# A fused two-block layer: the front of the first projection begun with three blocks in 48 pieces instead of two in 32, with one PSUM bank shared

## What is computed

```python
sc = jax.nn.silu(c)
scc = jax.nn.silu(c_ctx)
shift, scale, gate = jnp.split(sc @ w_ada[l] + b_ada[l], 3, axis=-1)
shift_c, scale_c, gate_c = jnp.split(scc @ w_ada[l] + b_ada[l], 3, axis=-1)
hc = _rmsnorm(ctx, g_pre[l]) * (1.0 + scale_c) + shift_c
zc = hc @ (w_in[l][:, :XBC_W + DT_W] if last else w_in[l])
xh_c, B_c, C_c, dt_c, A = _ssd_prep(zc, conv_w[l], conv_b[l], dt_bias[l], a_log[l], 1, CTX_LEN)
hx = _rmsnorm(x, g_pre[l]) * (1.0 + scale[:, None]) + shift[:, None]
zx = hx @ w_in[l]
xh, Bm, Cm, dt, A = _ssd_prep(zx, conv_w[l], conv_b[l], dt_bias[l], a_log[l], ROWS, GRID_W)
```

## Time and profile before

| what | value |
|---|---|
| median of 3 runs | 2824.82 us (2823.69 to 2825.59) |
| profiled execution, its own time | 2825.9 us |
| its span, first to last instruction | 2824.1 us |
| PE busy | 2772.1 us (98%), 13174 matmuls |
| VectorE, ScalarE, GpSimd busy | 54%, 39%, 12% |
| DMA | 439.35 MB, mean 156 GB/s |
| first matmul of the body | 165.13 us |
| mean granted TensorE clock | 0.995 of full speed |

### The profile page before, as it was taken

The page is one execution under the profiler, slowest core; times in us unless marked ns, Lnnn a source line. Parts: engine busy times, 40 slices in busy tenths (PEclk is TensorE's granted clock), DMA queues, the critical chain, the costliest instruction groups (busy, mean ns, idle before and its releaser), DMA issues.

```text
span 2824.1 us, 33335 instructions
## 1 busy us (share of the span) xinstructions
PE 2772.1 (98%) x13174; PEld 2245.8 (80%) x13174; DVE 1530.3 (54%) x1834; ACT 1112.1 (39%) x1470; POOL 343.0 (12%) x409
## 2 busy tenths in 40 slices
PE   6999999999999999999999999899999999999999
PEld 2578888888778887888788888788878888788787
DVE  6868667764555546666653233544444444533643
ACT  6742222234343333433333332436555543432611
POOL 0211100000334124322311000100000000000000
PEclk8999999999999999999999999999999999999999
DMA  9657767754455554455455333242222223223252
GB/s 398 245 192 257 250 238 261 256 186 144 142 167 173 164 171 150 148 174 182 143 167 214 112 120 104 86 146 90 82 75 82 83 75 109 78 90 97 96 183 94
DMA packets 162122, 439.35 MB, mean 156 GB/s; under 512 B 14768, under 2 KB 59824, under 8 KB 151728
## 3 DMA queue, kind: packets, MB, share of 16 engines
q1 hardware_dynamic: 123360, 307.28, 32.5%
q0 software_dynamic: 15792, 92.99, 9.3%
q10 hardware_dynamic: 22816, 36.97, 3.7%
HBM read 398.11 MB, written 39.06 MB: 155 GB/s over the span
## 4 chain that ended last, share of the span: by engine, by line
PE 91%; DVE 3%; ACT 3%; issue 2%; DMA 1%; POOL 0%; SPq 0%; DVEq 0%; ACTq 0%
PE PB L413 16%; PE PB L418 15%; PE PB L419 15%; PE PB L522 10%; PE PB L523 10%; PE PB L524 10%; PE PB L416 2%; PE PB L417 2%; PE PB L421 2%; ACT WH L1001 1%; PE PB L639 1%; PE PB L656 1%; PE PB L433 1%; DVE WL L1628 1%; PE PB L886 1%
## 5 line engine op out<-in xcount | busy, mean ns | idle before, releaser
L1628 DVE TENSOR_TENSOR WL<-RAW,WH 128x1024 fp32r<-128x1024 f32 (+1 forms) x424 | 519.5, 1233 | 765.2 <-ACT WH L1001 579.7
L413 PE MATMUL PB<-HH,WH 128*128 128x512 f32 x2048 | 818.9, 400 | 4.1 <-ACT zp L1001 3.7
L418 PE MATMUL PB<-HL,WH 128*128 128x512 f32 x2048 | 802.3, 392 | 0.0
L419 PE MATMUL PB<-HH,WL 128*128 128x512 f32 x2048 | 801.5, 391 | 0.0
L1001 ACT ACTIVATE WH<-RAW 128x1024 fp32r<-128x1024 f32 (+1 forms) x424 | 432.8, 1038 | 434.3 <-PE PB L524 259.8
L522 PE MATMUL PB<-WH,HH 128*128 128x512 f32 x1248 | 490.6, 393 | 0.8 <-DVE HL L1628 0.8
L524 PE MATMUL PB<-WH,HL 128*128 128x512 f32 x1248 | 486.2, 390 | 0.0
L523 PE MATMUL PB<-WL,HH 128*128 128x512 f32 x1248 | 486.1, 390 | 0.0
L413 PEld LDWEIGHTS PB<-HH,WH 128*128 128x128 f32 x2048 | 385.0, 188 | 93.7 <-issue 7.8
L419 PEld LDWEIGHTS PB<-HH,WL 128*128 128x128 f32 x2048 | 385.2, 188 | 67.1
L418 PEld LDWEIGHTS PB<-HL,WH 128*128 128x128 f32 x2048 | 385.6, 188 | 65.5 <-issue 3.4
(11 more groups left out here) (314 smaller groups left out, 2810.0 us busy)
## 6 DMA issues: line engine op xcount, KB each, us to landing
RAW<-in_w_in_t SPq DMA_DIRECT2D x320, 512.0 KB, 3.7
AU<-in_w_ada POOLq DMA_DIRECT2D x64, 1024.0 KB, 5.5
RAW<-in_w_out_t SPq DMA_DIRECT2D x96, 512.0 KB, 3.6
bcb<-R SPq DMA_DIRECT2D x64, 256.0 KB, 6.1
S<-so ACTq DMA_DIRECT2D x24, 384.0 KB, 2.7
ebc<-R SPq DMA_DIRECT2D x32, 256.0 KB, 6.0
SY<-evb ACTq DMA_DIRECT2D x32, 256.0 KB, 2.6
yin<-SY POOLq DMA_DIRECT2D x32, 256.0 KB, 4.3
```

The lines of the kernel that those rows point to most:

```text
L413: h.matmul(banks[j], lh, m.HH[:, t, :], start=st, stop=False)
L418: h.matmul(banks[j], lh, m.HL[:, t, :], start=False, stop=False)
L419: ins = h.matmul(banks[j], ll, m.HH[:, t, :], start=False, stop=en)
L1628: return h.tensor_tensor(o, a, b, op)
```

## The change

The front now begins three blocks without ctx (12, 13, 14) in 48 pieces, 1.5 a beat; the order of blocks becomes 12 to 15, then 0 to 11, so that the last is one with ctx. The first body block is 15, whose first two units are 12 and 13. The six accumulators take banks 0 to 5, the row sums bank 7, and **bank 6 is shared** by fold, x turned and ctx turned, each waiting for what read it last. ctx is turned two tiles at a time, in beats 19, 20, 23, 24, 27, 28, 31 and 35; ScalarE modulates both and splits off the high parts, VectorE makes the low parts, GpSimd none. Early halves are split one beat ahead of use instead of two. SyncE issues 12 raw units among the loads of w_ada, unit u at w_ada tile 6 + 16u/3. The table of places is rewritten to fit. The core of the diff:

```diff
-BLOCKS = (12, 13) + tuple(range(12)) + (14, 15)
-EARLY = 8
+BLOCKS = (12, 13, 14, 15) + tuple(range(12))
+LAST = BLOCKS[15]
+EARLY = 12
...
-    return st, t, k - 20 if 20 <= k < 36 else None, k - 6 if 6 <= k < 6 + 4 * EARLY else None
-BEATS = 6 + 4 * EARLY
+    j = k - 6
+    pieces = range((3 * j + 1) // 2, (3 * j + 4) // 2) if 0 <= j < 32 else range(0)
+    return st, t, {19: 0, 20: 1, 23: 2, 24: 3, 27: 4, 28: 5, 31: 6, 35: 7}.get(k), pieces
+BEATS = 38
...
-    u, tt = divmod(s, 4)
-    return u, tt % 2, tt, 2 * u + tt // 2
+    return s // 4, s % 3, s % 4, s // 3
...
     def fold(st):
+        bank = reuse(6)
         P.wait_ge(*at("rowb", st))
         P.wait_ge(*at("cst"))
-        if st:
-            P.wait_ge(*at("mod", st - 1))
...
-        freed[4] = [("mod", st)]
+        freed[6] = [("mod", st)]
...
+        freed[6] = [("hx", t)]
-    def turn_ctx(t):
+    def turn_ctx(c):
+        bank = reuse(6)
         for v in range(4, 6):
             P.wait_ge(*at("xs", v))
+        for q in range(4):
+            t, v = 2 * c + q // 2, q % 2
+            ins = h.transpose(bank[:, q * 128:(q + 1) * 128], m.xs[4 + v][:, t * 128:(t + 1) * 128], ident)
+        ins.then_inc(*put(P.side, "turn ctx", c))
+        freed[6] = [("hc", 2 * c + 1)]
...
-            if i < 2:
+            if i < 3:
                 continue
...
+    def modulate_ctx(c):
+        A.wait_ge(*at("turn ctx", c))
+        A.wait_ge(*at("Am", c))
+        for t in (2 * c, 2 * c + 1):
+            if t >= 2:
+                A.wait_ge(*at("CL", t - 2))
+            A.then(act(m.hf[t % 2][:, 512:768], m.PB[6][:, t % 2 * 256:t % 2 * 256 + 256], ACT.Identity,
+                       scale=m.Amv[:, t, 1:2], bias=m.modv[:, shift_at(t), 1:2]), "hc", t)
+        place_read(6 * (c // 2) + 4)
+        for t in (2 * c, 2 * c + 1):
+            A.wait_ge(*at("hc", t))
+            A.then(act(m.CH[:, t, :], m.hf[t % 2][:, 512:768], ACT.Copy), "CH", t)
...
-    make(8)
-    make(9)
+        if k in (33, 34):
+            make(k - 21)
...
+    def ctx_low(c):
+        for t in (2 * c, 2 * c + 1):
+            place_read(6 * (t // 4) + 5)
+            V.wait_ge(*at("CH", t))
+            V.then(TT(m.CL[:, t, :], m.hf[t % 2][:, 512:768], m.CH[:, t, :].bitcast(F32), ALU.subtract), "CL", t)
...
     for i in range(64):
-        if i % 8 == 6:
-            raw_load(i // 8)
+        for u in range(EARLY):
+            if i == min(6 + 16 * u // 3, 63):
+                raw_load(u)
```

More of the change, by code:

```diff
@@ L481, in tensor_program @@
             fold(st)
-        if sub is not None:
+        for sub in pieces:
             u, i, tt, t = early_tile(sub)
@@ L564, in tensor_program @@
         with_ctx = b < 12
-        tk = early[i] if i < 2 else [take(ring, "xbc", b, j) for j in range(3 if with_ctx else 2)]
+        tk = early[i] if i < 3 else [take(ring, "xbc", b, j) for j in range(3 if with_ctx else 2)]
         for k4 in range(4):
-            if i < 2:
+            if i < 3:
                 continue
@@ L1062, in scalar_program @@
     for k in range(BEATS):
-        st, t, tc, sub = beat(k)
+        st, t, tc, pieces = beat(k)
         for i in (2 * k, 2 * k + 1):
@@ L1076, in scalar_program @@
                 junk = A.then(act(m.junk, m.xs[v], ACT.Square, acc=m.ss[:, v:v + 1]), "x squared", v)
-        sub = beat(k + 2)[3]
-        if sub is not None and sub % 2 == 0:
-            early_high(sub)
-    make(8)
-    make(9)
+        for sub in beat(k + 1)[3]:
+            if sub % 2 == 0:
+                early_high(sub)
+        if k in (33, 34):
+            make(k - 21)
     def conv_out(i):
@@ L1726, in vector_program @@
                 a_low(i + 2)
+            if tc is not None and i % 2:
+                ctx_low(tc)
             if i in SCALED:
@@ L1730, in vector_program @@
                 V.then(TS(m.xs[v], m.xs[v], m.rr[:, v:v + 1], None, ALU.mult), "xs", v)
-        sub = beat(k + 2)[3]
-        if sub is not None and sub % 2 == 0:
-            early_low(sub)
-    make(8)
-    make(9)
-    for e in ("turn", 15), ("turn ctx", 15), ("HL", 15), ("CL", 15), ("fold", 7):
+        for sub in beat(k + 1)[3]:
+            if sub % 2 == 0:
+                early_low(sub)
+        if k in (33, 34):
+            make(k - 21)
+    for e in ("turn", 15), ("turn ctx", 7), ("HL", 15), ("CL", 15), ("fold", 7):
         V.wait_ge(*at(*e))
@@ L2318, in gpsimd_program @@
         power(rr, "rr", v)
-    for t in range(16):
-        i = max(i for i in range(64) if PLACE[i] == 6 * (t // 4) + 5)
-        G.wait_ge(*at("a hi", i))
-        G.wait_ge(*at("a lo", i))
-        G.wait_ge(*at("CH", t))
-        G.then(h.tensor_tensor(m.CL[:, t, :], m.hf[t % 2][:, 512:768], m.CH[:, t, :].bitcast(F32), ALU.subtract),
-               "CL", t)
-    for e in ("turn", 15), ("turn ctx", 15), ("HL", 15), ("CL", 15), ("fold", 7):
+    for e in ("turn", 15), ("turn ctx", 7), ("HL", 15), ("CL", 15), ("fold", 7):
         G.wait_ge(*at(*e))
@@ L2512, in sync_program @@
             load(m.xs[v], m.x_tile(I, v), s.x[v], "x", v)
-    for u in range(8, 68):
+    for u in range(EARLY, 68):
         raw_load(u)
```

70 lines of the change are left out of this document (25 added, 45 removed).

## The result

| | before | after |
|---|---|---|
| median (6 runs each) | 2824.26 us (2823.69 to 2825.59) | **2836.05 us** (2833.34 to 2848.82) |
| ratio, 95% interval | | 1.0048 (1.0029 to 1.0068) |
| profiled execution, its span | 2825.9, 2824.1 us | 2840.4, 2838.6 us |
| mean granted TensorE clock | 0.995 | 0.990 |

The change makes the kernel slower by 0.48%. The median lies within the range of 2822 to 2840, and on the side to which I had given 0.43, not on that of the likeliest case.

The account below looks back on a forecast made before the run. PE, busy 98% of the span, was taken to bound the kernel. Net +3.7 us at the first ctx block and +1.0 at the stage's end gave +4.7, a forecast median of 2829.5 us, range 2822 to 2840.

Parts of the forecast that it names:

- likeliest case: Whole kernel: hidden 22 us given back in front growth and the wait for unit 14, no difference that shows; chance 0.50.
- rival 2: Front: shared bank binds harder through ScalarE, folds and x's turns wait longer, 9.5 us more, 2839 us; chance 0.36.
- the body's first block: Body start: PE waits 12.2 us on unit 14, ready 24.2 us after first eviction; first ctx block net +3.7 us.
- stages without a gap: Front, fold to fold where PE never idles: six pieces instead of four are paid in full, +2.8 us.
- double ctx beats: Front, fold 5 to 6 and 6 to 7: stages grow to 19.0 to 19.2 us, +2.4 us each.
- fold waits: Front, shared bank: the fold waits 1.1 us for ScalarE's ctx work, at three folds.
- Fold 4 to fold 5: Front stage there: turn waits 2.7 us behind VectorE's scalings, fold 1.1; stage 21.4 to 21.6 us, +3.6.
- the hand-over: Fold 8 to the first eviction: 14.1 us instead of 16.8, -2.7 us, with no gap or clock loss on PE.
- rival 3: SyncE's gated loads land late, each of four gates costs 4 to 5 us: +16 to +20, some 2846; chance 0.07.
- The end of the stage: Last block before dt: three steps of the ada sums drained at once, PE waits about 1 us in all.
- The clock behind the wait on unit 14: Body's first block: PE restarts at the lower clock after the wait, costing 1.7 us.
- Rival 4: Faster: front gaps absorb pieces and fold waits are nil, -2 us; -14 (2811) only with unit 14 split sooner; chance 0.07.

Follow-up runs that it names:

- r0_after: The changed kernel itself, unaltered, run again as the measure for other follow-up runs; 2840.27 us, ratio 1.0049 to the kernel before.
- e9_phase: Changed kernel with six steps of the ada sums instead of four in the body's first block (15); 2833.20 us, ratio 1.0029.
- e2_ada: Changed kernel with four more steps of the ada sums in mid-body blocks, none left for the last block; 2845.78 us, ratio 1.0073.
- e4_scale: Changed kernel with VectorE's two scalings of ctx two beats later, beat 18 instead of 16; 2832.13 us, ratio 1.0026.
- e3_bank: Kernel before, plus only the shared bank 6 and ctx in pairs on ScalarE, low parts on VectorE; 2828.12 us, ratio 1.0009.
- e1_split: Changed kernel with units 14 and 15 split earlier on ScalarE and VectorE; 2838.17 us, ratio 1.0042.
- e8_four: Changed kernel with units 14 to 17 split one by one between the evictions, not behind the third; 2833.08 us, ratio 1.0027.

## Why the prediction was right, and where it failed

That the median fell in the range is in part luck. The forecast of 2829.5 was 6.6 us too low (9.8 by the profiled executions), and the range reaches 2840 only because of rival 2, whose mechanism didn't come.

- **What bounds, and where the hidden work goes: right.** The step "the body's first block" had a wait of 12.2 us on unit 14's low part, 24.2 us behind the first eviction; it was 11.9 and 24.1. The stages without a gap cost +2.7 for +2.8, those with double ctx beats 18.97 and 19.07 for 19.2, fold waits 1.02 for 1.1, the turn's wait 2.5 for 2.7. The modulation of 256 columns took 0.55 us on ScalarE, between the bounds and as taken.

```profile
L1001 ACT ACTIVATE hf<-PB,small 128x256 f32<-128x256 f32 x16 | 8.0, 554 | 2.8 <-PE PB L466 2.8
```

- The rule that I weighed against it (the Trainium skill, "Trainium Architecture — The Big Picture", "The five engines, in one table": VectorE up to about three times as fast per element) doesn't show here: 554 ns against VectorE's 535, both reading PSUM.
- **Fold 4 to fold 5: undersized by 1.6 us** in the profiled execution, by 0.1 in r0_after. I had priced the wait and left out that the clock may fall behind it, though I had charged that to the wait at the hand-over.
- **The hand-over: undersized by 1.6.** "The chain of h tiles 14 and 15, the last ctx pair and the last early half" took every operand as there. ScalarE waited 1.44 us on the raw tile of unit 13 (174.57 above), whose load SyncE issued at 171.21, right behind the last split of unit 10 (its low part ran on VectorE from 170.45), with the DMA engines busy for 0.24 from 167 to 174. SyncE's loads were a small cost, at a place where I hadn't looked for it; rival 3's waits in beats 10 to 20 didn't come.
- **"The end of the stage", "about 1 us in all": the step that failed**, by 6.3 us. I counted only the three drained steps (and four fewer ahead of the last block, where the programs have six: 70 of 76). By starting one block without ctx earlier, the change moves all 76 steps against the blocks: the third sum's last step then stood behind both halves of a convolution on VectorE and in the same unit as PE's use of it, where before it stood ahead of the convolution. e9_phase moved the steps back and got 7.7 us; e2_ada moved them to a worse place and lost 5.5. How long PE waits in the moved place depends on when a load lands (e4_scale).
- **The clock behind the wait on unit 14: undersized by 0.7.** The 1.7 us were read behind the kernel before's idle time of 3.7 us; behind 11.9 us it was 2.4.
- **The likeliest case (no difference, 0.50): wrong**, by these four terms. **Rival 2**, on the right side and with nearly the right time (2839), was wrong in its mechanism: the folds didn't wait 2 us longer each, and e3_bank gives the bank, with the ctx part, 2.8 us (5.5 in the stages, 3.0 of it won back at the hand-over). **Rival 4**'s sentence that splitting unit 14 sooner gives 14 us fell in e1_split: 2 us.

## What to carry to other kernels

Work hidden in a gap of PE can be given back at the first engine behind it that has no slack: here VectorE, in whose queue each wait taken away showed the next. Where side work advances in fixed steps beside a loop, moving the loop's start shifts every step against the loop's body, and a wait can appear hundreds of microseconds away; count the steps to each of its sums before and after. Price a wait of PE with the fall of the clock behind it, as a chance where it is short.

## What the runs showed of the hardware

- TensorE's clock fell to its lower level around waits as short as 1.88 us (e8_four, at 508.75; 0.53 from 512 to 520 us) and 2.06 us (after; 0.66 from 515 to 520), and around the same wait of 2.51 us at 93 us in one execution (0.65) and not in another (1.00). The same wait thus had two prices, which is part of the scatter of the change's runs (2833.3 to 2848.8).
- A VectorE subtraction of 512 columns with both operands in SBUF took 1110 ns in the kernel before, where GpSimd subtracted ctx low parts beside it, and 682 ns in the change, where GpSimd did nothing there. From 100 to 165 us, before, then after:

```profile
L1628 DVE TENSOR_TENSOR WL<-RAW,WH 128x512 fp32r<-128x512 f32 x8 | 8.9, 1110 | 2.2 <-ACT WH L1001 2.2
```

```profile
L1636 DVE TENSOR_TENSOR WL<-RAW,WH 128x512 fp32r<-128x512 f32 x11 | 7.5, 682 | 0.0
L1636 DVE TENSOR_TENSOR CL<-hf,CH 128x256 fp32r<-128x256 f32 x14 | 5.2, 406 | 0.0
```

In the kernel before, too, it was 685 ns (mean of 8) from 40 to 100 us, where GpSimd had no ctx low part yet. The eight slow ones cost 3.4 us together; that pays about half of the 16 low parts of ctx that VectorE took over (406 ns each, 6.5 us). By the Trainium skill ("SBUF — State Buffer", "SBUF: two separate sides"), VectorE with two SBUF inputs and a GpSimd operation that reads SBUF exclude each other for a whole instruction; these rows agree: GpSimd's own subtractions took 0.73 us at the least and up to 2.92 beside VectorE's. I hadn't counted it.
